# Expert 0's first two matrices beside the end of the second pass, and block 0's rows fetched there

## The reference

```python
h = x + concat(mlstm_heads, chunk_mlp) @ w_out
xf = rmsnorm(h)
g_sel = argmax(xf @ rg_w + rg_b)                      # 1 of 4 groups
top_v, top_i = top_k(e_logits of that group, 2)       # 2 of its 8 experts
weights = g_w * softmax(top_v)
y = sum over both experts of w * ((silu(xf @ w1[e]) * (xf @ w3[e])) @ w2[e])
h = h + y
h = h + sigmoid(h @ w_pg) * rmsnorm(p @ w_ple)
```

## Time and profile before

| | |
|---|---|
| median of 3 runs | 2302.97 us (2302.84 to 2303.97) |
| profiled execution | 2305.2 us, span 2303.6 |
| mean granted TensorE clock | 0.970 |
| TensorE busy | 2183.3 us, 95% of the span |
| VectorE, ScalarE, GpSimd busy | 1487.3, 974.8, 416.4 us |
| DMA | 407.12 MB, mean 177 GB/s |

### The profile page before, as it was taken

The page is one execution under the profiler, slowest core; times in us unless marked ns, Lnnn a source line. Parts: engine busy times, 40 slices in busy tenths (PEclk is TensorE's granted clock), DMA queues, the critical chain, the costliest instruction groups (busy, mean ns, idle before and its releaser), DMA issues. The chain is left out here.

```text
span 2303.6 us, 33708 instructions
## 1 busy us (share of the span) xinstructions
PE 2183.3 (95%) x10675; PEld 1797.0 (78%) x10676; DVE 1487.3 (65%) x2860; ACT 974.8 (42%) x1569; POOL 416.4 (18%) x571
## 2 busy tenths in 40 slices
PE   6999999999899999994789999999999999989998
PEld 5888888888688888883678888878888887867775
DVE  4787778777646666554554557686665666855564
ACT  4433343334332222221444455575555555733332
POOL 1121101010234333332110000000000000033332
PEclk9999999999899999997899999999999999999999
DMA  6111101122634433221795759697775778944431
GB/s 226 58 37 65 64 35 61 64 74 75 205 101 110 146 124 136 101 78 58 287 371 199 279 182 368 215 398 290 291 293 181 294 287 338 343 149 148 155 131 54
DMA packets 160332, 407.12 MB, mean 177 GB/s; under 512 B 18836, under 2 KB 22348, under 8 KB 160015
## 3 DMA queue, kind: packets, MB, share of 16 engines
q1 hardware_dynamic: 138518, 337.17, 40.8%
q0 software_dynamic: 14560, 43.11, 5.5%
q10 hardware_dynamic: 7200, 26.22, 2.8%
HBM read 330.12 MB, written 84.82 MB: 180 GB/s over the span
## 5 line engine op out<-in xcount | busy, mean ns | idle before, releaser
L227 PE MATMUL bank<-w_hi,mix_x 128*128 128x512 f32 x816 | 337.1, 413 | 7.2 <-DVE w_lo L210 3.3
L2110 DVE TENSOR_TENSOR w_lo<-raw,w_hi 128x2048 fp32r<-128x2048 f32 x132 | 296.5, 2286 | 49.2 <-ACT w_hi L2046 49.2
L229 PE MATMUL bank<-w_hi,mix_x 128*128 128x512 f32 x816 | 327.7, 402 | 0.0
L228 PE MATMUL bank<-w_lo,mix_x 128*128 128x512 f32 x816 | 326.3, 400 | 0.0
L2011 PE MATMUL bank<-w_hi,x_hi 128*128 128x512 f32 x784 | 305.9, 390 | 2.1 <-DVE x_lo L2102 2.1
L2013 PE MATMUL bank<-w_hi,x_lo 128*128 128x512 f32 x784 | 305.7, 390 | 0.0
L2012 PE MATMUL bank<-w_lo,x_hi 128*128 128x512 f32 x784 | 305.7, 390 | 0.0
L2046 ACT ACTIVATE w_hi<-raw 128x2048 fp32r<-128x2048 f32 x132 | 247.1, 1929 | 25.9 <-DMA raw<-in_w 25.7
L227 PEld LDWEIGHTS bank<-w_hi,mix_x 128*128 128x128 f32 x816 | 159.3, 195 | 40.4 <-issue 4.0
L229 PEld LDWEIGHTS bank<-w_hi,mix_x 128*128 128x128 f32 x816 | 158.0, 194 | 35.3
L228 PEld LDWEIGHTS bank<-w_lo,mix_x 128*128 128x128 f32 x816 | 159.3, 195 | 31.0
(11 more groups left out here) (306 smaller groups left out, 4115.6 us busy)
## 6 DMA issues: line engine op xcount, KB each, us to landing
raw<-in_w SPq DMA_DIRECT2D x128, 1024.0 KB, 10.0
shared<-in_w SPq DMA_DIRECT2D x64, 1024.0 KB, 9.4
y_dram<-y_sb ACTq DMA_DIRECT2D x50, 512.0 KB, 6.8
xT_dram<-mix_x SPq DMA_DIRECT2D x34, 512.0 KB, 3.5
mix_x<-xT_dram SPq DMA_DIRECT2D x34, 512.0 KB, 4.5
shared<-in_w_in SPq DMA_DIRECT2D x24, 512.0 KB, 5.7
small<-in_x_prompt SPq DMA_DIRECT2D x16, 512.0 KB
xr_sb<-in_x_prompt SPq DMA_DIRECT2D x16, 512.0 KB
```

The costliest lines, as they stand in the source:

```text
L227: pe.matmul(bank[:, :], x_hi[:, k, :], wh[:, k, :], start=(k == 0), stop=False)
L228: pe.matmul(bank[:, :], x_hi[:, k, :], wl[:, k, :], start=False, stop=False)
L229: ins = pe.matmul(bank[:, :], x_lo[:, k, :], wh[:, k, :], start=False, stop=(k == KD - 1))
L2110: dve.tensor_tensor(w_lo[slot(j, m)][:, cols], raw[m][:, cols], w_hi[slot(j, m)][:, cols].bitcast(F32), ALU.subtract).then_inc(lo_ready, 1)
```

## The change

Eight pieces of 512 KB, four of expert 0's w1 and four of its w3, are now loaded and split in the second pass. Pieces 0 to 2 are loaded and split in step 15, and pieces 3 to 7 in step 16. They use five buffers that are free by then: the first three 4 KB of `shared`, and `gt` and `ge` of the gelu. `ge` is free last, so piece 4 is loaded last and waits for the mix of tile 16, while pieces 5 to 7 use the first three buffers again.

At the end of the pass GpSimd loads the first 128 entries of the list into `tok` and gathers block 0's rows into `hn`, the place that is `rows_in` in the experts. In the experts SP waits for those rows, then loads w2 of expert 0 and what follows. The splits of w1 and w3 are replaced by adding 4 to both counters, and the thresholds of the list's and rows' counters are raised by one transfer. GpSimd waits for the early rows and for their transposes before it starts its loop, which is not changed. The declarations of four semaphores move to the top.

```diff
@@ -124,6 +124,10 @@
         dve_const = sem("dve_const")
         turn = sem("turn")
+        hi_ready = sem("hi_ready")
+        lo_ready = sem("lo_ready")
+        entry_loaded = sem("entry_loaded")
+        rows_loaded = sem("rows_loaded")
@@ -1114,6 +1118,37 @@
                                           ALU.subtract).then_inc(o_lo, 1)
 
+                    flat = lambda x: x[:, :, :].rearrange("p a n -> p (a n)")
+                    AHEAD = 8
+                    ahead = [shared[:, 0:D], shared[:, D:2 * D], shared[:, 2 * D:3 * D], flat(gt), flat(ge)]
+                    a_raw = [sem(f"a_raw{i}") for i in range(len(ahead))]
+                    a_hi, a_lo = sem("a_hi"), sem("a_lo")
+                    def quarter_of(bank, q):
+                        return bank[q // 4][:, q % 4 * D:(q % 4 + 1) * D]
+                    def load_ahead(sp_, q):
+                        n = len(ahead)
+                        if q >= n:
+                            sp_.wait_ge(a_lo, q - n + 1)
+                        elif q == 3:
+                            sp_.wait_ge(gelu_ready, NTILE)
+                        elif q == 4:
+                            sp_.wait_ge(mix_ready, NTILE)
+                        k = 2 * (q % 4)
+                        sp_.dma_start(ahead[q % n].rearrange("p (k n) -> p k n", k=2),
+                                      a[("w1", "w3")[q // 4]][0, 0, k * P:(k + 2) * P, :].rearrange("(k p) n -> p k n", p=P)).then_inc(a_raw[q % n], 16)
+                    def ahead_hi(act, q):
+                        act.wait_ge(a_raw[q % len(ahead)], 16 * (q // len(ahead)) + 16)
+                        act.activation(quarter_of(w_hi, q), ahead[q % len(ahead)], ACT.Copy).then_inc(a_hi, 1)
+                    def ahead_lo(dve, q):
+                        dve.wait_ge(a_hi, q + 1)
+                        dve.tensor_tensor(quarter_of(w_lo, q), ahead[q % len(ahead)], quarter_of(w_hi, q).bitcast(F32), ALU.subtract).then_inc(a_lo, 1)
                     A, B, SS, Q = PS[2], PS[3], PS[4], [PS[5], PS[6]]
@@ -1190,10 +1225,17 @@
                                         sp_.wait_ge(d_ha_kept, 16)
                                     load_ha(u + 1, r_next)
+                                if r_next == NS:
+                                    for q in range(3):
+                                        load_ahead(sp_, q)
                                 sp_.wait_ge(h_ready, u + 1)
...
                                     load_rows(u + 1, r_next)
                                 sp_.dma_start(h_dram[bass.ds(u * P, r), :], h_sb[0:r, :]).then_inc(h_stored, 16)
+                                if r_next == NS:
+                                    for q in (3, 5, 6, 7):
+                                        load_ahead(sp_, q)
+                                    load_ahead(sp_, 4)
@@ -1442,8 +1484,13 @@
                                 if not r_next:
                                     hn_halves(u - 1, r_last)
+                                    for q in range(3, AHEAD):
+                                        ahead_hi(act, q)
                                 if past(u, 0):
                                     routing_exps(u - 1, r_last)
+                                if r_next == NS:
+                                    for q in range(3):
+                                        ahead_hi(act, q)
                                 if r_next:
@@ -1645,6 +1692,9 @@
                                     norm_h(u - 1, r_last)
                                 mix_rest(u, r)
+                                if not r_next:
+                                    for q in range(3, AHEAD):
+                                        ahead_lo(dve, q)
                                 if past(u, 0):
@@ -1652,7 +1702,12 @@
                                 if r_next:
                                     gelu_w3(u + 1, r_next)
+                                    if r_next == NS:
+                                        ahead_lo(dve, 0)
                                     gelu(u + 1, r_next)
+                                    if r_next == NS:
+                                        ahead_lo(dve, 1)
+                                        ahead_lo(dve, 2)
                                     norm_v(u + 1, r_next)
@@ -1849,9 +1904,13 @@
                             scatter(NT, NS)
                             hold(pool, scattered, 32 * NTILE)
-            hi_ready = sem("hi_ready")
-            lo_ready = sem("lo_ready")
+                            pool.dma_start(tok[:, :], list_dram[0:P, :]).then_inc(entry_loaded, 16)
+                            hold(pool, hn_stored, 16 * NTILE)
+                            hold(pool, hn_tp, NTILE)
+                            hold(pool, entry_loaded, 16)
+                            pool.indirect_dma_start(out=hn[:, :], out_offset=None, in_=hn_dram[0:NT * P + NS, :],
+                                                    in_offset=bass.IndirectOffsetOnAxis(ap=tok[:, 0:1], axis=0)).then_inc(rows_loaded, 16)
             late_loaded = sem("late_loaded")
@@ -1932,6 +1991,10 @@
                     return e * PARTS + m
 
+                def loads_until(e, m):
+                    return e + 1 if m == 2 else e
                 with nc.Block() as block:
@@ -1949,9 +2012,9 @@
                                     load(e, m, c)
 
-                        for m in range(PARTS):
-                            for c in range(2):
-                                load(0, m, c)
+                        sp_.wait_ge(rows_loaded, 16)
+                        for c in range(2):
+                            load(0, 2, c)
                         reload(1)
@@ -1979,16 +2042,19 @@
                             at = at if isinstance(at, int) else nc.s_assert_within(at, 0, NE * CAP - P)
                             pool.dma_start(entry[:, :], list_dram[bass.ds(at, P), :]).then_inc(entry_loaded, 16)
-                            hold(pool, entry_loaded, 16 * i + 16)
+                            hold(pool, entry_loaded, 16 * i + 32)
                             hold(pool, xe_tp, i + 1)
...
                                                     in_offset=bass.IndirectOffsetOnAxis(ap=entry[:, 0:1], axis=0)
                                                     ).then_inc(rows_loaded, 16)
-                            hold(pool, rows_loaded, 16 * i + 16)
+                            hold(pool, rows_loaded, 16 * i + 32)
 
...
                             gather(i, e * CAP + (i - first) * P)
 
+                        hold(pool, rows_loaded, 16)
+                        hold(pool, xe_tp, 2)
                         all_blocks(pool, block_of, None)
@@ -1997,7 +2063,7 @@
                     def _(pe):
                         def transposes(i):
-                            pe.wait_ge(rows_loaded, 16 * i + 16)
+                            pe.wait_ge(rows_loaded, 16 if isinstance(i, int) else 16 * i + 32)
                             for k in range(KD):
@@ -2053,7 +2119,7 @@
 
                             for c in range(2):
-                                act.wait_ge(raw_loaded[m][c], 16 * e + 16)
+                                act.wait_ge(raw_loaded[m][c], 16 * loads_until(e, m))
                                 cols = slice(c * PART // 2, (c + 1) * PART // 2)
@@ -2082,9 +2148,9 @@
 
                         act.sem_inc(y_stored, 16)
-                        split(0, 0, 0)
+                        act.sem_inc(hi_ready, 4)
                         x_halves(0)
-                        for part in ((0, 0, 1), (0, 0, 2), (1, 1, 0)):
+                        for part in ((0, 0, 2), (1, 1, 0)):
                             split(*part)
@@ -2128,9 +2194,9 @@
                                 split(*part)
 
-                        split(0, 0, 0)
+                        dve.sem_inc(lo_ready, 4)
                         x_halves(0)
-                        for part in ((0, 0, 1), (0, 0, 2), (1, 1, 0)):
+                        for part in ((0, 0, 2), (1, 1, 0)):
                             split(*part)
```

4 lines of the change are left out of this document (2 added, 2 removed).

## The result

The change makes the kernel slower: 2312.76 us (median of 6 runs, 2312.3 to 2318.04) against 2303.36 before (6 runs beside it, 2300.94 to 2307.17), a ratio of 1.0041 with a 95% interval of 1.0029 to 1.0053, so 6.7 to 12.2 us, 9.4 by the ratio. I had forecast +4.9, with +1 to +9 (2304 to 2312) as the forecast's own range and 2314 as the upper end of the wide one: the median lies 0.8 above the first and inside the second. The span of the profiled execution is 2311.3, 7.7 longer than before.

The account below looks back on a forecast made before the run. TensorE, busy 95% of the span, was taken as the bound. Steps +2.3, second transposes 4.7 later in all, and +0.2 behind them gave +4.9: 2307.9 us against 2302.97, own range 2304 to 2312, wide range 2297 to 2314.

Parts of the forecast that it names:

- The bound, and the first gap: TensorE, busy 95%, bounds; its 24.8 us wait between second pass and experts shrinks to about 12 to 14.
- What the change leaves in place.: GpSimd's loop fetches block 0 again, so two gathers precede TensorE's second transposes: 13 to 18 us wait, 4.7 later.
- short gathers: Rival: GpSimd's transfers before the second transposes do not suffer from the load burst; 6.2 us earlier, time 2297.0; chance 0.20.
- the repeated fetch costs nothing: Rival: counts or loop were misread, so the 10.7 us gain at the first transposes stands whole; 2292.3; chance 0.08.
- The sizes of the gathers: Between first and second transposes: list 5.5 and rows 7.7 us for block 0's copy, 5.5 and 5.8 for block 1's.
- The separation of the passes waits for GpSimd's request and not for the landing, so it is covered.: At the second pass's end: the barrier adds nothing to block 0's early gather, first transposes gain 10.7 us.
- The steps: Loading and splitting pieces in steps 15 and 16 costs +2.3 us together, at best +1.4, at worst +5.
- Step 15: Three ScalarE copies make the tanh of tile 16 late, and the chain behind it: +1.4 us.
- in its wait for GpSimd's root, so they add nothing of their own: Step 15: VectorE's second and third subtractions fit in its wait for GpSimd's root, at no cost.
- Step 16: Five pieces, load of the late one 7 us: VectorE 1.2 late at routing, 0.3 given back at the residual, +0.9.
- Behind the second transposes: TensorE resumes at 1.2 GHz, some 1.9 us slower, against a 1.45 wait for hid gone: net +0.2.
- the third rival: Long gathers (6.1 and 8.1 us) throughout and a late step 16, steps at +5: +11.5 us, 2314.5; chance 0.12.

Follow-up runs that it names:

- r1_once: The change with GpSimd's loop starting at block 1, so block 0 is fetched once: 2299.09 us against 2304.55 before, ratio 0.9974.
- r8_held: The change with SP waiting for block 1's rows between expert 0's w2 and expert 1's first load: 2312.88 us, one run, beside 2302.05 before.
- r9_rows_after: As r1_once, but block 0's rows are asked for behind the separation of the passes: 2299.56 us against 2305.34 before, ratio 0.9977.
- r2_steps: The kernel before plus the eight pieces loaded and split in steps 15 and 16, result unused: 2308.95 us against 2304.55, ratio 1.0017.
- r5_ahead_order: The change without early row fetch, block 0 fetched once, pieces reordered (copies around the tanh, piece 4 split last): 2297.39 us against 2305.34 before, ratio 0.9964.
- r4_order: r2_steps with step 15's copies spread around the tanh and squares, and piece 4 split last in step 16: 2306.08 us against 2304.55 before, ratio 1.0001.
- r6_once_order: r1_once with the pieces reordered as in r4_order and block 1's list loaded ahead of the first transposes: 2295.26 us against 2305.34 before, ratio 0.9956.

## Why the prediction was right, and where it was not

- **The bound, and the first gap.** Right in kind: the gap shrank from 24.8 to 13.8, into the forecast 12 to 14.
- **"What the change leaves in place."** This decided the sign, and it held: three requests for rows ahead of the second transposes, a wait of 16.2 there (13 to 18 was forecast), the clock at 1.2 GHz behind it. r1_once takes the second fetch away alone and is 0.26% faster than before. The rivals "short gathers" and "the repeated fetch costs nothing" fall; r8_held shows that the first of them is what happens when the loads are away.
- **The sizes of the gathers.** Taken 5.5 and 7.7 for block 0's copy, 5.5 and 5.8 for block 1's; measured 5.8, 7.5, 4.9 and 7.0. From the first transposes to the second I had 32.3, it was 33.1: 0.8 missed.
- **The step that failed: "The separation of the passes waits for GpSimd's request and not for the landing, so it is covered."** It waits for the landing, through the drain (6.0 us with the gather under way, 2.9 without, r9_rows_after), and opens 1.7 behind it. First transposes 14.4 behind the last matmul instead of the 12.4 of my sum: 2.0.
- **The steps: +2.3 was mis-sized, they cost 4.6 in this profile** (3.9 by the runs of r2_steps). The total lay inside my upper bound of +5, but by other terms than mine.
- **Step 15:** 1.4 forecast, 1.6 measured (A), which is near by luck. The tanh is only 1.0 late (2.95 behind the mark, 1.93 before). The other 0.6 are a term that the prediction put at nothing: the two subtractions "in its wait for GpSimd's root, so they add nothing of their own". The first instruction of that root, before and after, and the subtractions beside it:

```profile
1041.06 0.19 POOL L241 TENSOR_SCALAR stat<-stat 8x4 f32<-8x4 f32 x1 [8.79 <-ACT junk L1417]
```

```profile
1037.70 2.34 DVE L1150 TENSOR_TENSOR w_lo<-shared,w_hi 128x1024 fp32r<-128x1024 f32 x2
1039.27 0.83 POOL L245 TENSOR_SCALAR stat<-stat 8x4 f32<-8x4 f32 x1 [9.77 <-ACT junk L1459]
```

It takes 0.83 instead of 0.19 and ends as the subtractions end, in all six kernels with the change's order. In the other order it is 0.19 again, and the last instruction of the root, beside the third subtraction, takes 0.48 instead of 0.22: the 0.3 by which A is longer than before there.

- **Step 16:** forecast at 0.9, it cost 3.0 (B and C together). The load of piece 4, issued at 1047.56, took 8.7 to land instead of 7 and was there 23.7 behind the mark, where my sum has 21.7. ScalarE waited 2.98 for it, VectorE ended its splits 29.5 behind the mark instead of 27.5, and the routing began at once (the three rows under the table above). The residual did not give back what I had counted on. The slow clock in B, 1.0 more than before, was in no term either, but it is covered by VectorE here and is no part of the loss.
- **Behind the second transposes:** +0.2 forecast, +0.6 measured.

The four misses add up: 2.0 + 2.3 + 0.8 + 0.4 = 5.5, which is 10.4 instead of 4.9, and 10.5 by the account above. All four have one sign, and the measured loss, 9.4, is nearly twice the forecast. It lies just outside the forecast's own range and 1.2 below the upper end of the wide one, which stood there for the third rival (2314.5). Of that rival one half came true, the late step 16, and the other did not: the gathers were of the forecast's size. So the sign and the mechanism were foreseen; that the wide range held is in part luck.

## What to carry to other kernels

Where a loop's first round is hoisted out of it, count that every engine's loop has lost that round: here one loop kept it, and 14.6 us came with it (47.6 against 33.0). GpSimd's drain at this barrier waited for the gather that was under way, so an early fetch there gained no more than the barrier let it; measure what the fetch is worth without being early (r5_ahead_order got -8.3 of the best -10.1 that way). And extra work in a tuned step is cheap or dear by its order: the same eight copies cost 3.9 us or nearly nothing, by whether the critical tanh and the latest load stand before or behind them. Work that is put into an engine's idle time can still slow the engine that it waits for (0.83 instead of 0.19 on GpSimd here).

## What the runs showed of the hardware that I had not expected

- GpSimd's drain at the barrier before the experts takes 2.8 to 2.9 us with none of its transfers under way, and 6.0 to 6.2 with a gather of 512 KB just issued; then the engines pass about 1.7 us after the rows have landed. The 2.8 are of this place: GpSimd's drains at the other barriers of the kernel before take 0.03 to 3.4.
- The granted clock's return after an idle stretch differs between executions of the same instructions: in the same place 3, 5 or 10 slow matmuls of 16 (r4_order, r5_ahead_order, r6_once_order), 1.5 us between the shortest and the longest.
- A small instruction of GpSimd (8x4) takes 0.83 us beside VectorE's subtractions of two 128x1024 operands and 0.19 without them, and ends within 0.1 us of the subtractions' end. The durations show that they go together; what holds it up was not tried.
- The lists of blocks 0 and 1 (512 bytes) land in 2.3 to 2.4 us on quiet DMA engines and in 4.8 to 6.7 beside 1 MB loads; their rows (512 KB) in 4.1 to 4.8 and in 7.0 to 8.4.
